# A diffusion step on one core: who applies the modulation to the second half of a turned tile in the output projection, VectorE or ScalarE

## The chip, the cores and the metric

The kernel runs on one core of one Trainium2 chip. The metric is the device time of one launch in microseconds (us), the median of several runs. The engines are TensorE (PE in the rows, PEld its weight loads), VectorE (DVE), ScalarE (ACT), GpSimd (POOL) and SyncE (SP, which issues the transfers).

## What is computed

One layer of a hybrid backbone on 128 context tokens and 1024 latent tokens of width 1024. Attention-like and Fourier parts give a mixed tensor of 1024 columns; then come the output projection, a residual, and an MLP. The part that matters here stands between the mixed tensor and the first MLP product:

```python
y = jnp.concatenate([o, y_fno], axis=-1) @ w_out
x = x + gt_m * _rmsnorm(y, g_post_mix)
h = _rmsnorm(x, g_pre_mlp) * (1 + sc_f) + sh_f
f = jnp.square(jax.nn.relu(h @ w_fc1)) @ w_fc2
x = x + gt_f * _rmsnorm(f, g_post_mlp)
```

`(1 + sc_f)` times the gain and `sh_f` depend on the column alone (and on whether a token is context or latent). The word *modulation* below means this multiply and add.

## The kernel before, in words

Each engine has a program of its own, written out by hand, and they meet in semaphores. The tokens are nine tiles of 128 (tile 0 is the context). Products are made in three passes of fp16 high and low parts, so a value that enters a product must first be split: the high part is the value rounded to fp16, the low part is the value less the high part.

PSUM has eight banks. Ring A (four banks) takes the products of the output projection, ring B (three banks) the turned tiles. A ring's bank is written again only when its reader has counted the last content as read.

**The output projection** runs in steps j = 0 to 10. In step j TensorE makes four products of 12 matmuls for tile j, `wo(0,j)` to `wo(3,j)`; the even ones are read out of PSUM by ScalarE (`put_even`, L1117), the odd ones are added on top by VectorE (`put_odd`, L2038). Around them, in the order of each engine's program:

- ScalarE in step j: `put_even(0,j)`, `high_y(j+2)` (L1103), `squares_x1(j-1)` (L886, two of 512 columns), `high_2(j-2)` (L1142, the high part of the two halves), `norm_x1(j-1)` (L1137), `put_even(2,j)`, `squares_y(j)` (L886 again).
- VectorE in step j: `put_odd(1,j)`, `low_y(j+2)` (L2016), `post(j-1)` (L2049 and L2052, the gate and the residual), `modulate_2(j-2)` (L2060 for the modulation of both halves, L2075 for the low parts), `put_odd(3,j)`. Steps 4 to 9 also hold work on the first MLP weights (L598, L627, L615 on ScalarE).
- TensorE turns tile j-2 in step j, after `wo(1,j)` (L1298, eight transposes into two banks of ring B, one for each half of the columns). Tokens lie along the columns of a bank afterwards, and the model's columns on the partitions, so that a scale and a shift of a block of 128 columns is one value a partition.
- GpSimd makes the reciprocal roots from the sums of squares.

The modulated halves go through two buffers, `tb2[0]` (the trace calls it `region`) and `tb2[1]` (`ghb`). From them ScalarE writes the high part, and VectorE, which waits for that, the low part. The first MLP product `up(0,0)` needs the low parts of all nine tiles; its last two token blocks start when the semaphore `s_2l` has counted 18.

Of the kernel before, what the change touches and what calls it, by code (L numbers as in the profile page):

```python
# [6 lines left out]
ACT = mybir.ActivationFunctionType  # L7
# [6 lines left out]
P = 128  # L14
# [96 lines left out]
def hybrid_step(nc, a):  # L111
# [177 lines left out]
    with ExitStack() as ctx:  # L289
# [3 lines left out]
        def sem(name):  # L293
            return ctx.enter_context(nc.semaphore(name))
# [6 lines left out]
        B = Ring(banks[4:7], [sem(f"b_full{i}") for i in range(3)], [sem(f"b_free{i}") for i in range(3)], b_keys)  # L301
# [30 lines left out]
        def cols(n):  # L332
            used[0] += n
            assert used[0] <= SMALL
            return small[:, used[0] - n:used[0]]
# [4 lines left out]
        shf = [cols(16) for _ in range(2)]  # L340
        amul = [cols(16) for _ in range(2)]
# [57 lines left out]
        tb2 = [R5[:, 4096:4608], ghb[:]]  # L399
# [23 lines left out]
        s_2l = sem("h2_low")  # L423
# [451 lines left out]
        def _(act):  # L875
            own = Steps(act, s_act)
# [52 lines left out]
            for b in range(TB):  # L929
                for h in range(2):  # L930

                    for k in (4 * h + 2, 4 * h + 3):
                        for v, toks in block_parts(b):
                            c = 2 * k + v
                            own.did(nc.scalar.activation(xT[:, k, toks], xT[:, k, toks], ACT.Identity,
                                                         scale=amul[0][:, c:c + 1], bias=shf[0][:, c:c + 1]))
# [7 lines left out]
            def take_z(key):  # L944
                return A.take(act, key)
# [30 lines left out]
            for i in range(G_A):  # L976
                chunk_high(act, i + 1)
                if i == LR:
                    for key in z_uses(i):
                        bank = take_z(key)  # L980
                        t = key[3]
                        nc.scalar.activation(lrS[:, TBW * t:TBW * t + TBW], bank[0:2 * RANK, 0:TBW], ACT.Copy,
                                             scale=wcof[0:2 * RANK, i % 8:i % 8 + 1]).then_inc(A.read(key), 1)
# [11 lines left out]
                else:  # L995
                    if i == V_A:
                        decay_exps(1)
                    for key in z_uses(i):
                        bank = take_z(key)
                        nc.scalar.activation(vN[:, key[3], CW * (i - V_A):CW * (i - V_A) + CW], bank[:, 0:CW], ACT.Copy,  # L1000
                                             scale=wcof[:, i % 8:i % 8 + 1]).then_inc(A.read(key), 1)
# [18 lines left out]
            for what, n in gate_events:  # L1020
# [4 lines left out]
                else:  # L1025
# [4 lines left out]
                    bank = take_z(key)  # L1030
# [6 lines left out]
            for i in range(4):  # L1037
                bank = A.take(act, ("dA", i))
                nc.scalar.activation(AB[:, i, :], bank[:], ACT.Copy).then_inc(A.read(("dA", i)), 1)
            bank = A.take(act, ("dA", 4))  # L1040
            nc.scalar.activation(A512, bank[0:1, 0:4 * NCOS], ACT.Copy).then_inc(A.read(("dA", 4)), 1)
            bank = A.take(act, ("dA", 5))
# [19 lines left out]
            for i in range(-1, 4):  # L1062
                bank = A.take(act, ("Q", i))
# [7 lines left out]
            bank = E.take(act, ("Y1", 4))  # L1071
# [13 lines left out]
            for s, j in enumerate(b_order):  # L1085
                if s + 1 < NT:
                    scores(b_order[s + 1], ("U", 1, j))
                bank = O.take(act, ("o", j))
# [48 lines left out]
                nc.scalar.activation(yN[:, j % 4, :], x1[:, j, :], ACT.Copy, scale=qrs[:, j:j + 1]).then_inc(s_2x, 1)  # L1137

            def high_2(j):
                for h in range(2):  # L1140
                    B.wait_read(act, ("x2", j, h))
                    nc.scalar.activation(HT2h[:, 4 * h:4 * h + 4, P * j:P * j + P],  # L1142
                                         tb2[h].rearrange("p (k t) -> p k t", k=4), ACT.Copy).then_inc(s_2h, 1)
# [6 lines left out]
            for j in range(NT + 2):  # L1150
                if j < NT:
                    put_even(0, j)
                if j + 2 < NT:

                    high_y(j + 2)
                if 1 <= j <= NT:
                    squares_x1(j - 1)
                if j >= 2:
                    high_2(j - 2)
                if 1 <= j <= NT:  # L1160
                    norm_x1(j - 1)
                if j < NT:
                    put_even(2, j)
                if j == 6:
                    chunk_high(act, ff_split)
                if j == NT:
                    chunk_high(act, ff_split + 1)
                if j < 2:
                    for q in range(4):
                        put_gates(4 * j + q)  # L1170
                if j < NT:
                    squares_y(j)
# [428 lines left out]
        def _(dve):  # L1601
            own = Steps(dve, s_dve)
# [35 lines left out]
            bank = A.take(dve, "vec")  # L1638
# [65 lines left out]
            def modulate(key, norm, j, h, buf):  # L1704

                bank = B.take(dve, key)
                v = 1 if j == 0 else 0
                for k in range(4):
                    c = 2 * (4 * h + k) + v
                    ins = V.tensor_scalar(buf[:, P * k:P * k + P], bank[:, P * k:P * k + P], amul[norm][:, c:c + 1],  # L1710
                                          shf[norm][:, c:c + 1], ALU.mult, ALU.add)
                    if k < 3:
                        own.did(ins)
                ins.then_inc(B.read(key), 1)
# [164 lines left out]
            for what, n in gate_events:  # L1879
# [5 lines left out]
                elif what == "U":  # L1885
# [4 lines left out]
                    j = f_order[n]  # L1890
# [12 lines left out]
            for i in range(-1, 4):  # L1903
                key = ("P", i)
                bank = A.take(dve, key)
# [7 lines left out]
                for n, (y, low, high) in enumerate(outs):  # L1913
                    own.did(V.tensor_tensor(y[:, :, 1:64], p[:, :, 1:64], q, low))
                    own.did(V.tensor_tensor(y[:, :, P - 1:64:-1], p[:, :, 1:64], q, high))
                    ins = V.tensor_copy(y[:, :, 0:NCOS:64], p[:, :, 0:NCOS:64])
# [5 lines left out]
            bank = A.take(dve, key)  # L1922
# [141 lines left out]
                ins.then_inc(B.read(key), 1)  # L2064

            def modulate_2(j):
                for h in range(2):
                    if j >= 1:
                        dve.wait_ge(s_2l, 2 * (j - 1) + h + 1)
                    modulate(("x2", j, h), 1, j, h, tb2[h])  # L2070
                for h in range(2):
                    B.wait_read(dve, ("x2", j, h))
                    dve.wait_ge(s_2h, 2 * j + h + 1)
                    tile_ = (slice(None), slice(4 * h, 4 * h + 4), slice(P * j, P * j + P))
                    V.tensor_tensor(HT2l[tile_], tb2[h].rearrange("p (k t) -> p k t", k=4), HT2h[tile_],  # L2075
                                    ALU.subtract).then_inc(s_2l, 1)
# [12 lines left out]
            for j in range(NT + 2):  # L2089
                if j < NT:  # L2090
                    put_odd(1, j)
                if j + 2 < NT:
                    low_y(j + 2)
                if 1 <= j <= NT:
                    post(j - 1)
                if j >= 2:
                    modulate_2(j - 2)
                for _, n in wo_late_scales(j):
                    set_scale(n)
                if j < NT:  # L2100
                    put_odd(3, j)
                if j in (4, 5):
                    chunk_max(dve, F + j - 4)
                if j == 6:
                    chunk_low(dve, F)
                if j == NT:
                    chunk_low(dve, F + 1)
                if j == 0:
                    for q in range(4, 8):
                        diagonals(q)  # L2110
# [67 lines left out]
            for n, j in last_tiles:  # L2178
# [4 lines left out]
                bank = B.take(dve, key)  # L2183
# [64 lines left out]
```

## Time and profile before

| | us |
|---|---|
| median of 3 runs | 1338.31 |
| lowest and highest | 1337.14, 1339.93 |
| profiled execution, its own time | 1342.97 |
| span of its trace | 1341.2 |
| PE busy in the span | 1250.0 |
| DVE busy | 774.5 |
| ACT busy | 425.7 |

The output projection lies between about 455 us and 593 us of the span, and the MLP fills the rest. The busy times are averages over stages with different limits; what a change in one stage is worth must be read from that stage.

### The profile page before, as it was taken

The numbers are of one execution on the slowest core, as the hardware profiler recorded it, in microseconds if no ns is written. First come the engines' busy times: TensorE is split into PE (matmuls) and PEld (weight loads), VectorE is DVE, ScalarE is ACT, GpSimd is POOL, SyncE is SP. The second block draws the span as 40 slices with busy tenths as digits, with TensorE's granted clock in tenths as the row PEclk, the third lists the DMA queues.
The fourth block names the chain that finished last, engine by engine and source line by source line (L and its number), as shares of the span: only waits on it lengthen the run. The fifth ranks groups of instructions, "written<-read, shape, count | busy, mean of one in ns | idle before, by whom it ended". The sixth has DMA issues, their size and how long they took to land.

```text
span 1341.2 us, 18877 instructions
## 1 busy us (share of the span) xinstructions
PE 1250.0 (93%) x7421; PEld 742.2 (55%) x7421; DVE 774.5 (58%) x1253; ACT 425.7 (32%) x736; POOL 129.7 (10%) x258
## 2 busy tenths in 40 slices
PE   2779999999896798989999999999999999999997
PEld 1545668887575454456645545545546556455443
DVE  3583674895488748775454454545444454544556
ACT  4464353322223455553311302303213113113022
POOL 1100000331122111212000000000000000000013
PEclk8689999999987799999999999999999999999999
DMA  9932112335331600101111120111111111110002
GB/s 275 317 132 62 32 32 72 99 126 189 96 98 36 232 0 0 33 32 64 32 45 51 32 63 33 61 34 32 63 33 64 32 64 32 32 63 32 32 32 110
DMA packets 70894, 97.24 MB, mean 73 GB/s; under 512 B 3093, under 2 KB 53402, under 8 KB 70810
## 3 DMA queue, kind: packets, MB, share of 16 engines
q1 hardware_dynamic: 70810, 96.04, 22.0%
q8 instruction: 63, 1.03, 0.3%
q14 instruction: 21, 0.17, 0.0%
HBM read 86.33 MB, written 9.70 MB: 72 GB/s over the span
## 4 chain that ended last, share of the span: by engine, by line
PE 55%; DVE 1%; ACT 0%; issue 0%; POOL 0%; POOLq 0%; ACTq 0%; DVEq 0%
PE bank L1221 55%; DVE region L2060 0%; DVE ghb L2060 0%; ACT bank L886 0%; ACT whi L615 0%; DVE region L2173 0%; DVE region L2175 0%; POOL small L797 0%; DVE region L2049 0%; ACT region L1137 0%; ACT region L1142 0%; DVE region L2186 0%; DVE region L2075 0%; POOL small L795 0%; POOLq L289 0%
## 5 line engine op out<-in xcount | busy, mean ns | idle before, releaser
L1221 PE MATMUL bank<-whi,region 128*128 128x512 f16 (+1 forms) x1872 | 491.4, 348 | 5.9 <-ACT region L1117 4.5
L1221 PE MATMUL bank<-region,whi 128*128 128x384 f16 (+1 forms) x1872 | 459.4, 328 | 11.0 <-DVE wlo L627 11.0
L1221 PE MATMUL bank<-wlo,region 128*128 128x512 f16 (+1 forms) x936 | 326.1, 348 | 0.0
L1221 PE MATMUL bank<-region,wlo 128*128 128x384 f16 (+1 forms) x936 | 307.3, 328 | 0.0
L1221 PEld LDWEIGHTS bank<-whi,region 128*128 128x128 f16 x1872 | 184.3, 98 | 166.2 <-issue 9.2
L1221 PEld LDWEIGHTS bank<-region,whi 128*128 128x128 f16 (+1 forms) x1872 | 183.5, 98 | 133.5 <-DVE wlo L627 11.3
L2141 DVE SCALAR_TENSOR_TENSOR region<-bank,small,region 128x512 f32<-128x512 f32 x126 | 93.2, 749 | 158.8 <-PE bank L1221 158.4
L615 ACT ACTIVATE whi<-stage,small 128x2048 f16<-128x2048 f32 (+1 forms) x42 | 82.3, 1959 | 300.6 <-PE bank L1221 294.2
L1221 PE MATMUL bank<-region 128*128 128x512 f16 (+8 forms) x802 | 160.6, 372 | 17.2 <-DVE small L1611 5.4
L2123 DVE TENSOR_TENSOR region<-region 128x384 f32<-128x384 f32 x96 | 53.5, 557 | 182.0 <-ACT region L1189 182.0
L1221 PEld LDWEIGHTS bank<-region 128*128 128x128 f16 (+4 forms) x802 | 102.0, 164 | 66.5 <-issue 13.5
L1221 PEld LDWEIGHTS bank<-wlo,region 128*128 128x128 f16 x936 | 91.8, 98 | 78.0 <-issue 1.4
L1189 ACT ACTIVATE region<-bank,small 128x384 f32<-128x384 f32 x96 | 55.7, 580 | 232.3 <-PE bank L1221 230.9
L1221 PEld LDWEIGHTS bank<-region,wlo 128*128 128x128 f16 (+1 forms) x936 | 92.0, 98 | 61.5 <-issue 1.4
L627 DVE SCALAR_TENSOR_TENSOR wlo<-stage,small,whi 128x2048 f16<-128x2048 f32 (+1 forms) x42 | 96.6, 2299 | 13.2 <-ACT whi L615 13.2
L598 DVE TENSOR_REDUCE small<-stage 128x1 f32<-128x2048 f32 (+1 forms) x45 | 100.5, 2236 | 0.1
L886 ACT ACTIVATE bank<-region 128x512 f32<-128x512 f32 x72 | 43.2, 601 | 95.3 <-DVE region L2052 37.2
L1298 PE MATMUL bank<-consts,region 128*128 128x128 f32 x216 | 35.9, 318 | 28.3 <-ACT region L907 23.3
L2127 DVE TENSOR_TENSOR region<-region 128x384 f16<-128x384 f32 x96 | 53.6, 558 | 5.6
L1193 ACT ACTIVATE region<-region 128x384 f16<-128x384 f32 x96 | 50.3, 524 | 3.0
L1298 PEld LDWEIGHTS bank<-consts,region 128*128 128x128 f32 x216 | 30.4, 168 | 32.8 <-ACT region L907 18.5
L1611 DVE TENSOR_REDUCE small<-bank 128x1 f32<-128x128 f32 (+1 forms) x49 | 14.2, 289 | 46.8 <-PE bank L1221 46.7
(157 smaller groups left out, 900.6 us busy)
## 6 DMA issues: line engine op xcount, KB each, us to landing
stage<-in_w_fc SPq DMA_DIRECT2D x32, 1024.0 KB, 5.3
stage<-in_w_ada SPq DMA_DIRECT2D x16, 1024.0 KB, 5.4
region<-in_w_ada SPq DMA_DIRECT2D x8, 1024.0 KB, 12.3
stage<-in_w_in SPq DMA_DIRECT2D x8, 1024.0 KB, 5.4
x_with_position<-region SPq DMA_DIRECT2D x9, 512.0 KB, 5.7
region<-x_with_position SPq DMA_DIRECT2D x9, 512.0 KB, 7.7
region<-in_x_sample SPq DMA_DIRECT2D x8, 512.0 KB, 10.8
stage<-in_w_out SPq DMA_DIRECT2D x4, 1024.0 KB, 4.9
```

The costliest lines, as they stand in the source:

```text
L598: nc.vector.tensor_reduce(wmax[:, i % 8:i % 8 + 1], src, AX_X, ALU.max, apply_absolute_value=True).then_inc(s_wmax, 1)
L615: nc.scalar.activation(hi, src.rearrange("p (k n) -> p k n", n=hi.shape[-1]), ACT.Copy, scale=wscl[:, i % 8:i % 8 + 1]).then_inc(s_whi, 1)
L627: nc.vector.scalar_tensor_tensor(out=lo, in0=src.rearrange("p (k n) -> p k n", n=lo.shape[-1]), scalar=wscl[:, i % 8:i % 8 + 1], in1=hi, o ...
L886: nc.scalar.activation(sink[:, 0:width], src[:, width * h:width * h + width], ACT.Square, accum_out=out2[:, h:h + 1]).then_inc(done, 1)
L1189: nc.scalar.activation(frel[:, n_ % 2, :], bank[:, 0:TBW], ACT.Relu, scale=beta[:, 2 * (g % 2) + x:2 * (g % 2) + x + 1]).then_inc(A.read(k ...
L1193: nc.scalar.activation(FTh[g % 2][:, m, TBW * tb_:TBW * tb_ + TBW], frel[:, n_ % 2, :], ACT.Square).then_inc(s_fh, 1)
L1221: return nc.tensor.matmul(out, lhsT, rhs, start=start, stop=stop, skip_group_check=True)
L1298: ins = nc.tensor.transpose(bank[:, P * k:P * k + P], src[:, P * k:P * k + P], ident)
L1611: ins = V.tensor_reduce(out, bank[:, 0:P * n].rearrange("p (n q) -> p n q", n=n), AX_X, ALU.max)
L2123: V.tensor_tensor(fsq[:, n % 2, :], frel[:, n % 2, :], frel[:, n % 2, :], ALU.mult).then_inc(s_fq, 1)
L2127: V.tensor_tensor(FTl[g % 2][:, m, toks], fsq[:, n % 2, :], FTh[g % 2][:, m, toks], ALU.subtract).then_inc(s_fl, 1)
L2141: V.scalar_tensor_tensor(out=y, in0=bank[:], scalar=cof, in1=y, op0=ALU.mult, op1=ALU.add).then_inc(B.read(key), 1)
```

## The change

The four multiply-adds on the second half of each turned tile leave VectorE's `modulate_2` and become four ScalarE activations (`Identity` with a scale and a bias pointer), each on 128 columns read straight from the PSUM bank. They stand at the head of `high_2`, ahead of both high parts. VectorE keeps the first half and both low parts. ScalarE now waits for the turned bank itself, and from the second tile on for the low parts of the tile before (`s_2l`), since it writes over the buffer that they are made from.

```diff
             def high_2(j):
+                bank = B.take(act, ("x2", j, 1))
+                if j >= 1:
+                    act.wait_ge(s_2l, 2 * j)
+                for k in range(4):
+                    c = 2 * (4 + k) + (1 if j == 0 else 0)
+                    ins = nc.scalar.activation(tb2[1][:, P * k:P * k + P], bank[:, P * k:P * k + P], ACT.Identity,
+                                               scale=amul[1][:, c:c + 1], bias=shf[1][:, c:c + 1])
+                    if k < 3:
+                        own.did(ins)
+                ins.then_inc(B.read(("x2", j, 1)), 1)
                 for h in range(2):
                     B.wait_read(act, ("x2", j, h))
...
             def modulate_2(j):
-                for h in range(2):
-                    if j >= 1:
-                        dve.wait_ge(s_2l, 2 * (j - 1) + h + 1)
-                    modulate(("x2", j, h), 1, j, h, tb2[h])
+                if j >= 1:
+                    dve.wait_ge(s_2l, 2 * j - 1)
+                modulate(("x2", j, 0), 1, j, 0, tb2[0])
                 for h in range(2):
                     B.wait_read(dve, ("x2", j, h))
```

On ScalarE, step 2 of the output projection stood so before (L886 are the squares of `x1`, L1142 the high parts, L1137 the normed tile, L1117 `put_even(2,2)`):

```order
202 L886 ACTIVATE bank,small<-region 128x512 x2
203 L1142 ACTIVATE region<-region 128x4x128
204 L1142 ACTIVATE region<-ghb 128x4x128
205 L1137 ACTIVATE region<-region,small 128x1024
206 L1117 ACTIVATE region<-bank,small 128x512
```

The same place with the change (L1145 are the new activations, L1152 is what L1142 was):

```order
202 L886 ACTIVATE bank,small<-region 128x512 x2
203 L1145 ACTIVATE ghb<-bank,small 128x128 x4
204 L1152 ACTIVATE region<-region 128x4x128
205 L1152 ACTIVATE region<-ghb 128x4x128
206 L1137 ACTIVATE region<-region,small 128x1024
```

Four activations of 128 columns now stand between the squares and the high parts, and everything behind them on this engine moves back by four places; the same holds for each of the nine tiles.

On VectorE, step 2 held before, from the residual add (L2052) to `put_odd(3,2)` and `put_odd(1,3)` (L2038):

```order
423 L2052 TENSOR_TENSOR region<-region 128x1024
424 L2060 TENSOR_SCALAR region<-bank,small 128x128 x4
425 L2060 TENSOR_SCALAR ghb<-bank,small 128x128 x4
426 L2075 TENSOR_TENSOR region<-region 128x4x128
427 L2075 TENSOR_TENSOR region<-ghb,region 128x4x128
428 L2038 SCALAR_TENSOR_TENSOR region<-bank,small,region 128x512 x2
```

With the change (every line number is 9 or 10 higher: L2084 is what L2075 was, L2048 what L2038 was):

```order
423 L2062 TENSOR_TENSOR region<-region 128x1024
424 L2070 TENSOR_SCALAR region<-bank,small 128x128 x4
425 L2084 TENSOR_TENSOR region<-region 128x4x128
426 L2084 TENSOR_TENSOR region<-ghb,region 128x4x128
427 L2048 SCALAR_TENSOR_TENSOR region<-bank,small,region 128x512 x2
```

The four multiply-adds into `ghb` are gone, and nothing else has moved.

## Rows read from the trace of the kernel before

**Rows 1.** The profile page, part 1: busy us, share of the span, instructions.

```profile
PE 1250.0 (93%) x7421; PEld 742.2 (55%) x7421; DVE 774.5 (58%) x1253; ACT 425.7 (32%) x736; POOL 129.7 (10%) x258
```

**Rows 2.** The chain that ended last: start us, us, what.

```profile
593.26 738.57 PE bank L1221 x3996
```

**Rows 3.** Timeline of VectorE in the output projection: start us, us, instruction, idle before.

```profile
489.77 0.75 DVE L2038 SCALAR_TENSOR_TENSOR region<-bank,small,region 128x512 f32<-128x512 f32 x1 [6.12 <-PE bank L1221]
...
502.22 0.75 DVE L2038 SCALAR_TENSOR_TENSOR region<-bank,small,region 128x512 f32<-128x512 f32 x1 [2.24 <-ACT region L1117]
...
507.95 1.36 DVE L2060 TENSOR_SCALAR ghb<-bank,small 128x128 f32<-128x128 f32 x4
...
510.07 0.69 DVE L2075 TENSOR_TENSOR region<-ghb,region 128x512 f16<-128x512 f32 x1 [0.17 <-ACT region L1142]
511.68 0.75 DVE L2038 SCALAR_TENSOR_TENSOR region<-bank,small,region 128x512 f32<-128x512 f32 x1 [0.92 <-ACT region L1117]
514.67 0.75 DVE L2038 SCALAR_TENSOR_TENSOR region<-bank,small,region 128x512 f32<-128x512 f32 x1 [2.23 <-ACT region L1117]
...
541.08 0.75 DVE L2038 SCALAR_TENSOR_TENSOR region<-bank,small,region 128x512 f32<-128x512 f32 x1 [1.57 <-PE bank L1221]
```

**Rows 4.** Timeline of ScalarE in step 3 and at the start of step 4.

```profile
506.78 0.60 ACT L886 ACTIVATE bank<-region 128x512 f32<-128x512 f32 x1 [3.44 <-DVE region L2052]
...
508.17 0.61 ACT L1142 ACTIVATE region<-region 128x512 f16<-128x512 f32 x1
509.34 0.63 ACT L1142 ACTIVATE region<-ghb 128x512 f16<-128x512 f32 x1 [0.56 <-DVE ghb L2060]
509.87 1.13 ACT L1137 ACTIVATE region<-region,small 128x1024 f32<-128x1024 f32 x1
510.91 0.67 ACT L1117 ACTIVATE region<-bank,small 128x512 f32<-128x512 f32 x1
512.51 0.60 ACT L886 ACTIVATE bank<-region 128x512 f32<-128x512 f32 x1 [0.94 <-issue]
...
513.90 0.67 ACT L1117 ACTIVATE region<-bank,small 128x512 f32<-128x512 f32 x1
```

**Rows 5.** Timeline of TensorE: products of steps 2 and 3, and `wo(1,6)`.

```profile
490.44 5.34 PE L1221 MATMUL bank<-region 128*128 128x512 f16 x24
...
501.68 5.34 PE L1221 MATMUL bank<-region 128*128 128x512 f16 x24
...
536.61 0.38 PE L1221 MATMUL bank<-whi,region 128*128 128x512 f16 x1 [3.82 <-ACT region L1117]
```

**Rows 6.** ScalarE's groups with their shapes: count, busy us, mean ns of one.

```profile
L886 ACT ACTIVATE region<-bank 128x128 f32<-128x128 f32 x36 | 10.0, 277 | 52.0 <-PE bank L1221 51.2
...
L1031 ACT ACTIVATE region<-bank,small 128x256 f32<-128x256 f32 x18 | 8.5, 473 | 35.7 <-PE bank L1221 35.7
...
L935 ACT ACTIVATE region<-region,small 128x256 f32<-128x256 f32 x4 | 2.3, 585 | 0.0
L935 ACT ACTIVATE region<-region,small 128x128 f32<-128x128 f32 x4 | 1.9, 482 | 4.6 <-DVE small L1701 4.6
...
L615 ACT ACTIVATE whi<-stage,small 128x256 f16<-128x256 f32 x1 | 0.5, 492 | 0.0
```

**Rows 7.** Timeline of ScalarE at the first `Identity` activations of the kernel.

```profile
65.19 1.86 ACT L935 ACTIVATE region<-region,small 128x128 f32<-128x128 f32 x4 [4.60 <-DVE small L1701]
```

**Rows 8.** Timeline of both engines at the last tile.

```profile
589.11 1.36 DVE L2060 TENSOR_SCALAR region<-bank,small 128x128 f32<-128x128 f32 x4
...
592.51 0.69 DVE L2075 TENSOR_TENSOR region<-ghb,region 128x512 f16<-128x512 f32 x1 [0.17 <-ACT region L1142]
...
591.78 0.63 ACT L1142 ACTIVATE region<-ghb 128x512 f16<-128x512 f32 x1 [0.65 <-DVE ghb L2060]
```

**Rows 9.** Windows: each engine's busy us in a stretch, then the granted clock.

```profile
530.00:540.00 10.00, 6.18 (x23) 2.42 (x22) 8.91 (x17) 6.78 (x15) 1.74 (x6) 0.86 0.00 0
```

## The prediction

> **What bounds the kernel now.** I first read the busy shares on the page [rows 1]: TensorE is busy for 1250 of 1341 us. That would make any work on the other engines look free, so I then read the chain that ended last. From 593.26 us on it is one piece of TensorE, 738.57 us long [rows 2]: the MLP runs behind its first complete input without a gap that matters. So the end moves one for one with the moment at which the last low part of the last tile is there, and the question is what sets that moment.
>
> The timelines of the output projection answer it. TensorE needs 11.24 us for a step (501.68 less 490.44 [rows 5]). VectorE takes 12.45 us from one `put_odd(1,j)` to the next (514.67 less 502.22 [rows 3]), and nearly all its idle time there ends with ScalarE. ScalarE in turn idles 3.44 us before its squares until VectorE's residual add is through [rows 4]. Neither engine is full; together they form a ring of waits that is slower than TensorE. It runs in step 3 as follows. `put_odd(1,3)` starts at 502.22; behind it come the low parts of `y` and `post`, and ScalarE's squares start at 506.78: 4.56 us. The two squares take 1.39 us, up to 508.17. The two high parts take 1.70 us, up to 509.87, because the second waits 0.56 us for VectorE's second modulation [rows 4]. The normed tile takes 1.04 us, `put_even(2,3)` to the start of `put_odd(3,3)` 0.77 us, from there to the squares of `y` 0.83 us, these 1.39 us, and `put_even(0,4)` to the start of `put_odd(1,4)` again 0.77 us [rows 3, 4]. The sum is 12.45 us, the period. TensorE runs ahead of this ring until ring A is full: at 536.61 us it has stood 3.82 us for a bank that ScalarE must read [rows 5]. The ring of waits, then, is what the change must be weighed against.
>
> **The change part by part.**
>
> *Removed:* VectorE's four multiply-adds on the second half. They begin at 507.95 and last 1.36 us [rows 3]. By themselves they are on the ring, since the second high part waits for them; only that wait, 0.56 us in each step, can be won.
>
> *Added:* four activations of 128 columns out of PSUM with two pointers, on ScalarE between the squares and the high parts. The trace of before has no such row. The nearest is the same function with the same two pointers, 128 columns out of SBUF: 482 ns, and 585 ns for 256 columns [rows 6]. Four of these, two of each size in turn, took 1.86 us together [rows 7]; less the last one's 0.585 that leaves 1.275 us for three starts, of which one is 0.103 longer, so 0.39 us for one of 128 columns. Out of PSUM ScalarE is a little quicker: 256 columns with a scale pointer took 473 ns against 492 ns out of SBUF into fp16 [rows 6]. I take 0.37 us from start to start, 1.48 us for four. The bounds: the cheapest activation of 128 columns out of PSUM lasts 277 ns [rows 6]; with the same overlap of 0.09 it gives 0.19 and 0.75 us for four. The dearest is 0.482 without overlap, 1.93 us. My value stands near the upper one because the pointers do.
>
> *The step with the change:* the second high part no longer waits for VectorE; each takes 0.53 us from its start to the next (509.34 to 509.87 [rows 4]). From the squares' end to the normed tile it is now 1.48 + 1.06 = 2.54 us instead of 1.70: 0.84 us more in a step. The bounds are 0.75 + 1.06 - 1.70 = 0.11 and 1.93 + 1.06 - 1.70 = 1.29. The four activations are free of nothing: ScalarE idles 3.44 us ahead of the squares, with the turned bank ready, but its program has the new work behind the squares, and an engine takes its program in order. What queues behind them is the normed tile and `put_even(2,j)`; for these wait `put_odd(3,j)` on VectorE, the squares of `y`, `put_even(0,j+1)`, and after some steps TensorE, in ring A.
>
> *Counted:* the ring is entered in step 2, at a start that TensorE sets (489.77, idle 6.12 until a product [rows 3]) and that the change leaves alone. Steps 2 to 9 each carry one `high_2` ahead of a normed tile or, in step 9, ahead of the high part of the weights that VectorE needs next. That is 8 × 0.84 = 6.7 us later. TensorE's own start of `wo(1,6)` lies in between, but it is released by `put_even(2,5)` [rows 5], so it shifts with the ring.
>
> *Given back at the last tile:* in step 10 nothing else is left. Before, VectorE's eight multiply-adds start at 589.11 and TensorE goes on at 593.26, 4.15 us later [rows 2, 8]. Now ScalarE makes its half while VectorE is still at the weights. After VectorE's four (1.36), 0.03 and two high parts (0.53 to the second's start, 0.63 for it, as in the row at 591.78), 0.10 to the last low part and 0.75 from there to TensorE [rows 8, 2] give 3.40 us. That wins 0.75 us.
>
> *New waits:* the one on `s_2l` costs nothing. It asks for the low parts of the tile before, made in the step before (510.07 [rows 3]), while the new work of the next step starts behind the squares of that step, 10 us later. VectorE's first low part now waits for a later high part, but what stands behind it, `put_odd(3,j)`, waits even longer for `put_even(2,j)`.
>
> *Sum:* 6.7 - 0.75 = +6.0 us (bounds +0.1 and +9.6). The profiled execution would go from 1342.97 to 1349.0. It lies 4.66 us above the median of the runs, so I carry over only the difference: 1338.31 + 6.0 = **1344.3 us**. A change under 0.2% (2.7 us) is about what a measurement of this kernel can't tell from none.
>
> The Trainium skill, "ScalarE: Activation LUTs", section "What ACT_TABLE_LOAD costs", gives an activation 186 ns plus 0.833 ns a column, about 93 ns for each pointer and an overlap of 93 ns. An estimate from that page is 386 ns a start; the sum by it would be +6.5. The trace agrees in SBUF: 482 ns against the page's 479 [rows 6]. The same page, "Rules for kernel authors", says to keep multiply and add on VectorE. By that rule the change goes the wrong way, and the sum above has the same sign.
>
> **The rivals.**
>
> *The bias pointer costs nothing out of PSUM.* Then 473 ns less 103 for 128 columns is 0.37 us, 0.28 with the overlap, 1.12 us for four and 0.48 in a step [rows 6]: 8 × 0.48 - 0.75 = +3.1, 1341.4 us. Against it speaks the step from 492 to 585 ns at 256 columns in SBUF, where only a bias pointer and the output's type differ.
>
> *TensorE's clock.* The granted clock was 0.86 over 530 to 540 us, where TensorE had stood 3.82 us [rows 5, 9], and `put_odd(1,6)` then waited 1.57 us for a product [rows 3]. A later stall may fall otherwise. If this fall from 2.4 to 1.2 GHz doesn't come, up to 1.57 us is won: +4.4, 1342.7 us. If another stall brings one (TensorE will stand longer at several places), a product on the ring or the first products behind 593 us lose up to some 4 us: +10, 1348.3 us.
>
> *It ends on the other side: VectorE's relief goes through and ScalarE's work does not.* If the four activations cost under 0.64 us in all (0.16 each), the step gets shorter. At nothing it wins 0.64 us eight times and 0.75 once: -5.9, 1332.4 us. This would need them to run under the 3.44 us of idle, ahead of the squares. The ring, whose terms add up to the period, and the order of the program speak against it.
>
> *Nothing measurable:* an activation near the cheapest row gives +0.1; a free bias together with the clock's gain gives +1.5, 1339.8 us.
>
> **How the numbers follow.** Forecast 0.62; free bias 0.15; clock gain 0.05; clock loss 0.08; other side 0.04; nothing measurable 0.06. The range leaves out the last two and the far end of the clock loss: 1341.0 to 1347.5 us. Slower by over 0.2% are the forecast and three rivals less 0.02 for their near ends, 0.88; same 0.08; faster 0.04.
>
> **What would show it.** In the changed trace, four activations into `ghb` of some 460 ns in about 1.57 us, right behind ScalarE's squares, with no idle time before them; a period of about 13.3 us between the `put_odd(1,j)` of steps 3 to 5; ScalarE's wait for VectorE's `ghb` gone; TensorE at `wo(1,6)` near 540.0 us; the first product behind the last low part near 599.3 us instead of 593.26; the piece behind it as long as before. I am wrong if the period stays at 12.45 (the ring is not what I take it for), if the activations take under 0.3 us from start to start, or if TensorE's clock falls in another stretch than before.

## The result, and the profile after

| | before | changed |
|---|---|---|
| median, us | 1338.64 (6 runs, 1335.08 to 1340.33) | 1344.48 (6 runs, 1343.22 to 1347.57) |
| profiled execution | 1342.97 | 1345.24 |
| DVE busy | 774.5 | 763.0 |
| ACT busy | 425.7 | 438.0 |

The ratio is 1.0048, with a 95% interval of 1.0033 to 1.0062: the change costs 5.8 us of the median. VectorE lost 11.5 us of work and ScalarE gained 12.3 us, both far from full, and the kernel became slower.

The two profiled executions don't begin the output projection at the same time: `put_odd(1,2)`, whose start TensorE sets, stands at 489.77 us before [rows 3] and at 486.07 us after. So I compare stretches. From the start of `put_odd(1,2)` to TensorE's first product behind the last low part it was 489.77 to 593.26 before [rows 2, 3], 103.49 us. After, the timeline of VectorE shows the start, and TensorE's goes on at 595.26:

```profile
486.07 0.75 DVE L2048 SCALAR_TENSOR_TENSOR region<-bank,small,region 128x512 f32<-128x512 f32 x1 [6.13 <-PE bank L1231]
...
499.24 0.75 DVE L2048 SCALAR_TENSOR_TENSOR region<-bank,small,region 128x512 f32<-128x512 f32 x1 [2.24 <-ACT region L1117]
...
507.29 0.69 DVE L2084 TENSOR_TENSOR region<-region 128x512 f16<-128x512 f32 x1 [2.24 <-ACT region L1152]
...
509.43 0.75 DVE L2048 SCALAR_TENSOR_TENSOR region<-bank,small,region 128x512 f32<-128x512 f32 x1 [0.84 <-ACT region L1117]
512.42 0.75 DVE L2048 SCALAR_TENSOR_TENSOR region<-bank,small,region 128x512 f32<-128x512 f32 x1 [2.24 <-ACT region L1117]
```

The stretch is 109.19 us, 5.70 longer. The period is 13.18 us (512.42 less 499.24), where it was 12.45 [rows 3]. VectorE now idles 2.24 us for the high part; before, that wait was 0.17 us and four multiply-adds stood there [rows 3]. ScalarE in the same step 3:

```profile
503.80 0.60 ACT L886 ACTIVATE bank<-region 128x512 f32<-128x512 f32 x1 [3.44 <-DVE region L2062]
...
505.19 1.49 ACT L1145 ACTIVATE ghb<-bank,small 128x128 f32<-128x128 f32 x4
506.56 0.63 ACT L1152 ACTIVATE region<-region 128x512 f16<-128x512 f32 x1
...
507.60 1.15 ACT L1137 ACTIVATE region<-region,small 128x1024 f32<-128x1024 f32 x1
508.64 0.69 ACT L1117 ACTIVATE region<-bank,small 128x512 f32<-128x512 f32 x1
510.26 0.60 ACT L886 ACTIVATE bank<-region 128x512 f32<-128x512 f32 x1 [0.94 <-issue]
...
511.65 0.67 ACT L1117 ACTIVATE region<-bank,small 128x512 f32<-128x512 f32 x1
```

This answers to [rows 4]. The four activations stand behind the squares with no idle time between, and from the squares' end (505.19) to the normed tile (507.60) it is 2.41 us instead of 1.70. Each activation lasts 450 ns in the view of groups, and from the start of the first to the start of what follows the four take 1.37 us:

```profile
L1145 ACT ACTIVATE ghb<-bank,small 128x128 f32<-128x128 f32 x36 | 13.4, 450 | 0.0
```

The timeline of TensorE shows `wo(1,6)`, the turn of the last tile and, in its last row here, the product behind the last low part; the windows view shows the clock around the first two (column behind POOL):

```profile
535.83 0.58 PE L1231 MATMUL bank<-whi,region 128*128 128x512 f16 x1 [4.55 <-ACT region L1117]
...
587.64 1.69 PE L1308 MATMUL bank<-consts,region 128*128 128x128 f32 x8 [2.84 <-ACT region L1137]
589.12 5.18 PE L1231 MATMUL bank<-region 128*128 128x384 f16 x24
595.26 4.07 PE L1231 MATMUL bank<-region 128*128 128x384 f16 x24 [0.95 <-DVE region L2084]
```

```profile
530.00:540.00 10.00, 5.45 (x16) 1.85 (x15) 6.17 (x12) 8.73 (x19) 1.87 (x6) 0.67 0.00 1
...
580.00:590.00 10.00, 7.16 (x41) 4.54 (x40) 5.57 (x9) 7.33 (x14) 0.97 (x4) 0.90 0.00 0
```

Behind that product the two traces are about as long: 747.94 us to the end of the span before and 748.24 after.

### The profile page after: what moved, and what is told of

It reads as the page before. It is cut to its first block, busy times and chain, and to the rows that moved or that the text cites. A ratio compares the mean times of both kernels' runs of the same rounds, so it can differ in the third digit from the quotient of the medians.

```text
span 1343.5 us, 18877 instructions
## 1 busy us (share of the span) xinstructions
PE 1250.8 (93%) x7421; PEld 741.4 (55%) x7421; DVE 763.0 (57%) x1217; ACT 438.0 (33%) x772; POOL 129.9 (10%) x258
## 4 chain that ended last, share of the span: by engine, by line
PE 55%; ACT 1%; DVE 1%; issue 0%; POOL 0%; POOLq 0%; ACTq 0%; DVEq 0%
PE bank L1231 55%; ACT bank L886 0%; ACT whi L615 0%; ACT region L1137 0%; DVE region L2182 0%; ACT ghb L1145 0%; DVE region L2184 0%; DVE region L2070 0%; POOL small L797 0%; ACT region L1152 0%; DVE region L2059 0%; DVE region L2062 0%; DVE region L2084 0%; DVE region L2195 0%; POOL small L795 0%
## 5 line engine op out<-in xcount | busy, mean ns | idle before, releaser
L1231 PE MATMUL bank<-region,whi 128*128 128x384 f16 (+1 forms) x1872 | 459.9, 328 | 11.1 <-DVE wlo L627 11.1
L1231 PEld LDWEIGHTS bank<-whi,region 128*128 128x128 f16 x1872 | 184.4, 99 | 167.8 <-issue 11.1
L886 ACT ACTIVATE bank<-region 128x512 f32<-128x512 f32 x72 | 43.3, 601 | 94.7 <-DVE region L2062 37.7
## 6 DMA issues: line engine op xcount, KB each, us to landing
region<-in_w_ada SPq DMA_DIRECT2D x8, 1024.0 KB, 12.1
```

Source lines behind the costliest of these rows:

```text
L886: nc.scalar.activation(sink[:, 0:width], src[:, width * h:width * h + width], ACT.Square, accum_out=out2[:, h:h + 1]).then_inc(done, 1)
L1231: return nc.tensor.matmul(out, lhsT, rhs, start=start, stop=stop, skip_group_check=True)
```

## The experiments

The times of single runs of one kernel scatter over 10 us and more, so that an interval is 0.3 to 0.7% wide. I therefore read the stretch from the start of `put_odd(1,2)` to the product behind the last low part in each trace as well, and the period between two `put_odd(1,j)`, which repeats to 0.01 us.

| run | what | ratio to before (95%) | period, us | stretch, us |
|---|---|---|---|---|
| before | | 1 | 12.45 | 103.49 |
| changed | | 1.0048 (1.0033 to 1.0062) | 13.18 | 109.19 |
| e1_ahead | activations ahead of the squares | 1.0010 (0.9992 to 1.0029) | 12.61 | 103.82 |
| e3_ballast | idle work on VectorE | 1.0023 (0.9998 to 1.0048) | 13.17 | 109.95 |
| e8_twice | activations made twice | 1.0123 (1.0099 to 1.0147) | 14.57 | 120.77 |
| e9_last | change for the last tile alone | 0.9978 (0.9962 to 0.9993) | 12.46 | 102.79 |
| e7_ahead_wait | e1, low parts behind GpSimd | 0.9972 (0.9951 to 0.9992) | 12.07 | 98.72 |
| e4_order_before | kernel before, reads reordered | 0.9896 (0.9860 to 0.9933) | 11.23 | 93.44 |
| e5_order_after | changed, reads reordered | 0.9963 (0.9939 to 0.9986) | 12.12 | 100.53 |
| e6_order_ahead | e5, activations ahead of the squares | 0.9888 (0.9852 to 0.9925) | 11.23 | 92.44 |
| e10_order_last | e4, last tile on ScalarE | 0.9927 (0.9906 to 0.9948) | 11.23 | 92.80 |

The four kernels with reordered reads (e4, e5, e6, e10) start this stretch 0.57 us earlier against the first `put_odd(1,1)` (15.40 instead of 15.97 us between the two starts in e4 and in before), so that they win this on top. The stretch says nothing of what comes behind it: from its end to the end of the span it is 747.9 to 748.4 us in every trace but that of e7, where it is 749.88.

### Twice the suspected cost

```diff
+                own.settle()
+                for k in range(4):
+                    own.did(nc.scalar.activation(gex[:, k // 2, P * (k % 2):P * (k % 2) + P], bank[:, P * k:P * k + P], ACT.Identity,
+                                                 scale=amul[1][:, 8 + 2 * k:9 + 2 * k], bias=shf[1][:, 8 + 2 * k:9 + 2 * k]))
                 for k in range(4):
                     c = 2 * (4 + k) + (1 if j == 0 else 0)
```

> The changed kernel with ScalarE's four activations made twice in each tile, the extra four into a spare buffer, ahead of the real ones. Theory: 4 x 0.34 = 1.37 us more on the ring in each of the steps 2 to 9, nothing at the last tile, where they lie under VectorE's low part of the weights: period 14.55 us, 8 x 1.37 = +11.0 over the changed kernel, about +16.7 against before. Rival (a part of the +5.7 between the two traces is TensorE's clock at longer stalls): the step grows by 1.37 and the stretch by clearly more or less than 11.

The timeline of ScalarE, step 3, and after it the one of VectorE in the same run:

```profile
504.20 1.49 ACT L1145 ACTIVATE gex<-bank,small 128x128 f32<-128x128 f32 x4
505.57 1.51 ACT L1149 ACTIVATE ghb<-bank,small 128x128 f32<-128x128 f32 x4
506.94 0.66 ACT L1156 ACTIVATE region<-region 128x512 f16<-128x512 f32 x1
```

```profile
498.26 0.75 DVE L2052 SCALAR_TENSOR_TENSOR region<-bank,small,region 128x512 f32<-128x512 f32 x1 [2.24 <-ACT region L1117]
...
507.70 0.69 DVE L2088 TENSOR_TENSOR region<-region 128x512 f16<-128x512 f32 x1 [3.64 <-ACT region L1156]
...
512.83 0.75 DVE L2052 SCALAR_TENSOR_TENSOR region<-bank,small,region 128x512 f32<-128x512 f32 x1 [2.24 <-ACT region L1117]
```

The second four take 1.37 us like the first, and the period grew by 1.39, to 14.57. The stretch is 11.58 us longer than that of the changed kernel, where eight steps give 11.1. The ratio to before is 1.0123, some 16.5 us. So the cost is proportional to what stands on ScalarE between the squares and the normed tile, and what is left for the rival is under 0.5 us: 0.40 of it stands between `put_odd(1,5)` and `put_odd(1,6)`, around `wo(1,6)`.

### VectorE's relief taken away

```diff
                 modulate(("x2", j, 0), 1, j, 0, tb2[0])
+                own.settle()
+                for k in range(6):
+                    spare = gex[:, k // 2, P * (k % 2):P * (k % 2) + P] if k < 4 else part[k - 4][:, 0:P]
+                    own.did(V.tensor_scalar(spare, ident, amul[1][:, 2 * k:2 * k + 1],
+                                            shf[1][:, 2 * k:2 * k + 1], ALU.mult, ALU.add))
```

> The changed kernel with six idle multiply-adds of 128 columns (constants in, spare buffers out, 0.22 us each, 1.3 us together) on VectorE behind the modulation of the first half, so that VectorE is about as busy as before the change. Theory: VectorE's relief is worth nothing on the ring, since it idles 2.25 us there for the high part: period still 13.18 us; only at the last tile the idle time before the low part is 0.77 us, so that about 0.5 us comes out: +0.5 over the changed kernel, about 1345.0 us. Rival (the relief of VectorE is real and hides part of ScalarE's cost): up to 1.3 us in each of eight steps, about 1354 us.

VectorE's timeline, step 3:

```profile
504.29 0.75 DVE L2048 SCALAR_TENSOR_TENSOR region<-bank,small,region 128x512 f32<-128x512 f32 x1 [2.24 <-ACT region L1117]
...
510.01 1.11 DVE L2083 TENSOR_SCALAR gex<-consts,small 128x128 f32<-128x128 f32 x4
511.04 0.60 DVE L2083 TENSOR_SCALAR part<-consts,small 128x128 f32<-128x128 f32 x2
512.34 0.69 DVE L2089 TENSOR_TENSOR region<-region 128x512 f16<-128x512 f32 x1 [0.71 <-ACT region L1152]
...
517.46 0.75 DVE L2048 SCALAR_TENSOR_TENSOR region<-bank,small,region 128x512 f32<-128x512 f32 x1 [2.24 <-ACT region L1117]
```

The six took up 1.5 of the idle time ahead of the low part, which shrank from 2.24 to 0.71 us, and the period stayed at 13.17. The stretch grew by 0.76 us (expected 0.5). At the last tile it is 4.16 us from the modulation to TensorE's next product instead of 3.48, which is 0.68 of it, and 0.12 stands around `wo(1,6)`. So the work that left VectorE had been worth nothing to the changed kernel in the steps, and at the last tile it is worth all that the change wins there. The times alone, 1.0023 with an interval up to 1.0048, don't tell this run from the changed kernel or from before.

### The activations where ScalarE idles

```diff
                 if j >= 2:
+                    mod_2(j - 2)
+                if 1 <= j <= NT:
+                    squares_x1(j - 1)
+                if j >= 2:
                     high_2(j - 2)
```

> The changed kernel with one edit: ScalarE's four activations stand ahead of its squares of x1, where it idles 3.44 us in each step, and no longer behind them. Theory (a ring of waits between ScalarE and VectorE is the bound, and what counts is what stands on it): the four leave the ring. From the squares' end to the normed tile there is then either two high parts (1.04 us) or GpSimd's reciprocal root (squares end 508.17, the three GpSimd operations end near 509.45 in the trace of before, so about 1.31 us), whichever is longer: the period falls from 13.18 to about 12.1 us, 0.39 us under the kernel before, and the last tile keeps its gain of 0.67. Sum against before: 8 x -0.39 - 0.67 = -3.8, about 1334.8 us. Rival (the four cost their own time on ScalarE wherever they stand, or the loss comes from TensorE's stalls and clock): as the changed kernel, about 1344.5 us.

`mod_2` holds the four activations, which stood at the head of `high_2`. This one missed, between the two theories: 12.61 us for the period and not 12.1, and a ratio of 1.0010, where 3.8 us less than before had been expected. The timelines of GpSimd, VectorE and ScalarE of this run show a wait that I had not counted:

```profile
506.61 0.55 POOL L746 TENSOR_TENSOR small<-small 128x1 f32<-128x1 f32 x1
...
513.32 1.09 POOL L746 TENSOR_TENSOR small<-small 128x1 f32<-128x1 f32 x1
```

```profile
513.31 0.69 DVE L2088 TENSOR_TENSOR region<-region 128x512 f16<-128x512 f32 x1 [0.85 <-ACT region L1154]
513.92 0.69 DVE L2088 TENSOR_TENSOR region<-ghb,region 128x512 f16<-128x512 f32 x1
```

```profile
512.59 0.61 ACT L1154 ACTIVATE region<-region 128x512 f16<-128x512 f32 x1
...
514.44 1.15 ACT L1137 ACTIVATE region<-region,small 128x1024 f32<-128x1024 f32 x1 [0.72 <-POOL small L746]
```

ScalarE is through with both high parts and idles 0.72 us for GpSimd's reciprocal root. The power operation (L746) took 1.09 us at 513.32, beside VectorE's low part, which started at 513.31; the other one, at 506.61, took 0.55. So it is at all eight places of this trace where the two start within 0.01 us of each other (1.08 or 1.09 us). In the trace of before all nineteen power operations of the output projection take 0.55 to 0.58 us; a low part begins there while one runs, but only 0.3 us behind its start (in step 3 at 509.22, the power operation at 508.89). So a further run only kept them apart:

```diff
+                dve.wait_ge(s_qrs, min(j + 2, NT))
                 for h in range(2):
                     B.wait_read(dve, ("x2", j, h))
                     dve.wait_ge(s_2h, 2 * j + h + 1)
```

> The kernel with the four activations ahead of the squares (run e1_ahead), and with one wait more: VectorE's low parts wait until GpSimd has set the reciprocal root of x1. In e1_ahead the period was 12.61 us and not 12.1, and GpSimd's power operation (L746) took 1.09 us instead of 0.55 where VectorE's low part (two inputs from SBUF) started beside it. Theory (these two engines held each other up): with the low part behind it the power operation takes 0.55 us again, the normed tile starts 0.54 us earlier, period 12.07 us, 8 x -0.54 = -4.3 against e1_ahead, in all -3.9 us against before, from the first put_odd(1,1) to the product behind the last low part. Rival (the power operation is slow there for another reason, such as its place in time): still 1.09 us, period 12.6 us or more.

The timelines of GpSimd, VectorE and ScalarE in step 3, and TensorE's first products behind the last low part:

```profile
508.45 0.55 POOL L746 TENSOR_TENSOR small<-small 128x1 f32<-128x1 f32 x1
```

```profile
509.03 0.69 DVE L2089 TENSOR_TENSOR region<-region 128x512 f16<-128x512 f32 x1 [1.45 <-POOL small L746]
```

```profile
507.72 0.61 ACT L1154 ACTIVATE region<-region 128x512 f16<-128x512 f32 x1
...
509.03 1.15 ACT L1137 ACTIVATE region<-region,small 128x1024 f32<-128x1024 f32 x1 [0.18 <-POOL small L746]
```

```profile
588.42 5.64 PE L1235 MATMUL bank<-region 128*128 128x384 f16 x24 [2.66 <-DVE region L2089]
```

Again 0.55 us, and the normed tile starts 1.31 us behind the squares' end (509.03 less 507.72), the length of GpSimd's three operations with their hand-overs. The period is 12.07, as expected, and a wait that was added made the kernel faster. The rows of e1 fit the reading that the power operation is held until the first low part is nearly through and then takes its 0.55 us: it ends 1.10 us behind the low part's start (514.41 less 513.31). The same 1.10 us stands in e6 where a power operation started 0.21 us behind a low part and took 0.89:

```profile
541.86 0.89 POOL L746 TENSOR_TENSOR small<-small 128x1 f32<-128x1 f32 x1
```

```profile
541.65 0.68 DVE L2090 TENSOR_TENSOR region<-region 128x512 f16<-128x512 f32 x1
```

The Trainium skill, "GPSIMD Engine Reference", section "1. Specifications", gives GpSimd's SBUF interfaces as shared with VectorE, with contention for VectorE instructions that have two SBUF inputs; L2075 and its like have two, and the trace agrees (1.09 against 0.55 us). The stretch fell by 4.77 us against before, where eight steps at 0.38 and the last tile give 3.7. Against before, `put_odd(1,6)` also follows `put_odd(3,5)` by 2.99 us (538.00 less 535.01) instead of 4.52, because TensorE's stall ahead of `wo(1,6)` is 2.82 us here and its clock stays at 1.00 over 530 to 540 us. That is 1.5 us more. Step 7 gives its 0.38 back: VectorE's `post` waits there for GpSimd's root of `y` and starts 1.72 us behind `put_odd(1,7)` instead of 1.36. Behind the stretch this execution loses 1.9 us again: TensorE's clock falls behind its stall of 2.66 us (0.91 over 580 to 590 us), and the first 24 products take 5.64 us instead of 4.08. On the whole the two traces differ by some 2.8 us, and the times by 0.28%, some 3.8 us.

### The last tile alone

```diff
             def high_2(j):
+                if j == NT - 1:
+                    bank = B.take(act, ("x2", j, 1))
...
             def modulate_2(j):
-                for h in range(2):
+                for h in range(1 if j == NT - 1 else 2):
```

Under the new condition stand the four activations of the change; all other tiles are as before.

> The kernel before with the change made for the last tile alone: ScalarE modulates its second half, all other tiles stay with VectorE. Theory: periods as before (12.45 us), and from the end of VectorE's low part of the weights to TensorE's next product 3.48 us instead of 4.15: -0.67 us in the trace, too little for the times (-0.05%). Rival (the gain at the last tile comes from the whole pattern): 4.15 us as before.

VectorE's timeline at the end of the stage:

```profile
587.10 1.36 DVE L2070 TENSOR_SCALAR region<-bank,small 128x128 f32<-128x128 f32 x4
...
589.83 0.68 DVE L2085 TENSOR_TENSOR region<-ghb,region 128x512 f16<-128x512 f32 x1
```

From the start of the modulation (587.10) to TensorE's next product (590.58) it is 3.48 us instead of 4.15 [rows 2, 8]; the stretch is 0.70 us shorter. The times say 0.9978, with an interval that ends at 0.9993, just short of the 0.9995 that the trace accounts for. What the rest of that difference is stays open; the statement on the last tile rests on the trace.

### Opening the ring

```diff
                 if 1 <= j <= NT:
                     squares_x1(j - 1)
+                if j < NT:
+                    put_even(2, j)
                 if j >= 2:
                     high_2(j - 2)
                 if 1 <= j <= NT:
                     norm_x1(j - 1)
-                if j < NT:
-                    put_even(2, j)
...
                 if j < NT:
                     put_odd(3, j)
+                if j >= 2:
+                    low_2(j - 2)
```

`low_2` is the second half of `modulate_2`. The same edit was made to the kernel before (e4), to the changed kernel (e5), and to e1 (e6); e10 is e4 with ScalarE at the last tile alone.

> The kernel before (VectorE modulates both halves) in another order: ScalarE reads put_even(2,j) ahead of the high parts and the normed tile, and VectorE takes put_odd(3,j) between the modulation and the low parts. Theory: the high parts then run beside put_odd(3,j) and no longer ahead of it. The ring is squares 1.39, put_even 0.57, up to the second high part's start about 0.6 (it waits for VectorE's second half), high part 0.53, normed tile 1.04, squares of y 1.39, put_even(0) to put_odd(1) 0.77, to the squares 4.56: about 10.9 us, under TensorE's 11.24. TensorE becomes the bound of the steps, its stall of 3.82 us and its clock fall go away, and the last product of tile 8 ends some 11 us earlier; the work on the MLP weights in steps 4 to 7 gives some of it back. Between 7 and 11 us faster, about 1329.5 us. Rival (the ring is not what holds the steps, the order of the reads changes nothing): 1338.6 us.

> The changed kernel with the same reordering, the four activations still behind the squares, ahead of the high parts. Theory: the four (1.37 us) are on the ring in place of the wait for VectorE (0.6): 1.39 + 0.57 + 1.37 + 1.04 + 1.04 + 1.39 + 0.77 + 4.56 = 12.13 us, above TensorE's 11.24, so the ring stays the bound: 8 x (12.13 - 12.45) - 0.67 = -3.2 against before, about 1335.4 us, and some 6 us behind the reordered kernel of before. Rival: with the ring opened the place of the modulation no longer matters, and it ends within 1 us of the reordered kernel of before.

> The changed kernel with the reordering and the four activations ahead of the squares. Theory: the ring is 1.39 + 0.57 + 1.04 + 1.04 + 1.39 + 0.77 + 4.56 = 10.76 us, under TensorE's 11.24, as in the reordered kernel of before; the change of engine is then worth only what it wins at the last tile, 0.67 us: about 1328.8 us. Rival (ScalarE's load itself costs): slower than the reordered kernel of before by 2 us or more.

> The reordered kernel of before (run e4_order_before) with ScalarE modulating the second half of the last tile alone. Theory: it takes from e4_order_before the 0.67 us of the last tile and stands within 0.4 us of e6_order_ahead in the trace: from the first put_odd(1,1) to the product behind the last low part 108.2 us. Rival (e6_order_ahead, at 107.8 us, owes its lead to VectorE's lower load in all steps): no better than 108.8 us.

VectorE's timeline of e4 in step 3, and below it the `put_odd` rows of e5:

```profile
502.93 0.75 DVE L2038 SCALAR_TENSOR_TENSOR region<-bank,small,region 128x512 f32<-128x512 f32 x1 [2.29 <-PE bank L1221]
...
508.65 1.36 DVE L2060 TENSOR_SCALAR ghb<-bank,small 128x128 f32<-128x128 f32 x4
509.93 0.74 DVE L2038 SCALAR_TENSOR_TENSOR region<-bank,small,region 128x512 f32<-128x512 f32 x1
...
511.19 0.69 DVE L2077 TENSOR_TENSOR region<-ghb,region 128x512 f16<-128x512 f32 x1
514.16 0.75 DVE L2038 SCALAR_TENSOR_TENSOR region<-bank,small,region 128x512 f32<-128x512 f32 x1 [2.29 <-PE bank L1221]
```

```profile
501.03 0.75 DVE L2048 SCALAR_TENSOR_TENSOR region<-bank,small,region 128x512 f32<-128x512 f32 x1 [2.20 <-ACT region L1117]
...
513.15 0.75 DVE L2048 SCALAR_TENSOR_TENSOR region<-bank,small,region 128x512 f32<-128x512 f32 x1 [2.20 <-ACT region L1117]
```

In e4 VectorE works from 502.93 to 511.88 without idling, and then waits 2.29 us for TensorE and no longer for ScalarE. TensorE has no idle time at all between 528 and 560 us, where it stood 3.82 us before [rows 5], and its granted clock over 530 to 540 us is 1.00 instead of 0.86 [rows 9]. The stretch is 93.44 us, 10.05 less, and 10.62 from the first `put_odd(1,1)` (7 to 11 expected); the times say 13.9 us, with an interval from 9.0 to 18.8. In e5 both waits still end with ScalarE and the period is 12.12 (12.13 expected), the stretch 2.96 us under that of before and 3.53 from the first `put_odd(1,1)` (3.2 expected): there the same change of engine costs 7.1 us of the stretch, more than in the original order. In e6 it costs nothing: 11.23 us again, bound by TensorE, and 1.00 us less than e4 in the stretch, of which e10 has 0.64. Counted from the first `put_odd(1,1)`, e10 takes 108.20 us and e6 107.84, as expected, so that most of the lead of e6 is the last tile. The times put e4, e6 and e10 at 1327.97, 1326.85 and 1330.61 us, with intervals that overlap; which of the three is fastest is not settled by them, that each beats before and changed kernel is. The edit moves reads on two engines at once, on ScalarE and on VectorE, and no run shows what either does alone.

## Why the prediction was right

**The ring of waits.** Right, and shown by taking its terms apart. In the changed kernel's rows: `put_odd(1,3)` to the squares 4.56, squares 1.39, four activations 1.37, two high parts 1.04, normed tile 1.04, to `put_odd(3,3)` 0.79, to the squares of `y` 0.83, these 1.39, to `put_odd(1,4)` 0.77: 13.18 us. Doubling one term (e8) moved the period by that term, work off the ring (e3) moved it by nothing, and shortening the ring below TensorE's 11.24 (e4, e6) made TensorE the bound.

**The price of the activation.** I took 0.37 us from start to start and it was 0.343 (the 386 ns of the prediction's other estimate were further off), with 450 ns for one instead of some 460; out of PSUM it is 32 ns cheaper than the 482 ns out of SBUF [rows 6]. With high parts at 0.52 that makes +0.71 us from the squares to the normed tile, and another 0.02 stands between `put_even(2,3)` and `put_odd(3,3)` (0.79 instead of 0.77), so the step came to +0.73 us instead of +0.84. The rival of a free bias pointer (+0.48, from 0.28 us a start) lies clearly off.

**The count.** Eight steps at 0.73 are 5.8 us, less 0.67 at the last tile (0.75 forecast) 5.2; measured 5.70. Most of the rest stands at `wo(1,6)`: TensorE stood 4.55 us there instead of 3.82, the granted clock over 530 to 540 us was 0.67 instead of 0.86, and from `put_even(2,5)` to `put_odd(1,6)` it took 5.75 us (535.00 to 540.75) instead of 5.29. I had this as a rival of either sign; it came as a small loss inside the forecast. A second fall, behind a stall of 2.84 us ahead of the turn of the last tile, slowed 24 products from 4.06 to 5.18 us and cost nothing, since TensorE still waited 0.95 us for the last low part. e7 shows both sides of this rival at their size: about 1.5 us won where the fall at `wo(1,6)` did not come, and 1.9 us lost where one came behind the last low part, with nothing left there to hide it.

**The median.** 5.8 us, against 6.0 forecast: the price was a little too high (0.9 us over eight steps) and the clock's share missing (0.46), and the two in part cancel. That the number came out within 0.2 us is luck; the ring and the order of size are not.

**The signs.** With the 3.70 us by which the changed trace starts the stretch earlier added back, `wo(1,6)` stands at 539.53 us (540.0 foretold) and the product behind the last low part at 598.96 (599.3); the four activations follow the squares without idle time, in 1.49 us (1.57). One sign of being wrong did show: TensorE's clock fell in another stretch than before, 0.90 over 580 to 590 us, where it had been 1.00. It lay inside a wait and moved no term of the sum, so the sign was drawn too wide.

**Where the text was incomplete.** It gave 0.56 us as all that can be won of VectorE's part, and 0.64 in the rival with the other sign; 0.64 is the right one, since a high part that need not wait starts 0.08 us before the one ahead of it ends. The rival with the other sign priced ScalarE's work at nothing and came to -5.9 us. It could not have reached that: e1 and e7 put the work where ScalarE idles, and then GpSimd's root is the next to be late, 1.31 us behind the squares, so that a step wins at most 0.38 and not 0.64 us. I named no engine that would be late next on that side.

## What to carry to other kernels

When two engines hand tiles to and fro, add up one turn of their waits and see whether it gives the period; only then does it show which work is on the path, and moving work to the emptier engine can lengthen it. Here the better answer was the order: reading the next product out of PSUM before the work that waits for the other engine brought the turn under TensorE's own period and won 1%. Who modulates is then worth under 1 us if the activations stand where ScalarE idles (e6), but 7.1 us if they stay behind the squares (e5): the place in the program counts for more than the engine. A short operation on a third engine can be the next to be late, and which instruction runs beside it can double its time.

## What the runs showed of the hardware

- GpSimd's power operation on one column took 0.55 us, and 1.09 us where VectorE's subtraction with two SBUF inputs started with it or up to 0.01 us ahead of it (e1, eight times), and 0.89 where it started 0.21 us behind the subtraction (e6); each of these ends about 1.10 us behind the subtraction's start. With a wait that kept them apart it was 0.55 again (e7), and where the subtraction started 0.33 us behind the power operation both kept their time, 0.68 and 0.55 us (before).
- An activation of 128 columns with a scale and a bias pointer takes 450 ns out of PSUM in the changed kernel (450 to 458 in the other traces, 475 for the second four of e8) against 482 ns out of SBUF before, and the next starts 343 ns behind it.
- TensorE's clock fell behind an idle time of 2.84 us in the changed kernel (windows 580 to 590: 0.90) and did not behind one of 2.82 us ahead of `wo(1,6)` in e7 (530 to 540: 1.00); it fell behind one of 2.66 us in e7 (580 to 590: 0.91) and did not behind one of 3.30 us before (590 to 600: 1.00). So the last idle time alone does not decide it.
